# Gate and up products taken apart for the first and the last unrolled expert of a layer, and the output stored from two queues

## The reference

```
eid, gate = hier_route(x2, w_rg, b_rg, w_re, b_re)      # 32 experts, two for each token
# per expert e, on the rows routed to it:
h = silu(xb @ w_gate[e]) * (xb @ w_up[e])               # 1024 -> 512, twice
y = h @ w_down[e]                                       # 512 -> 1024
out[token] += gate * y
```

## Time and profile before

| | us |
|---|---|
| median of 3 runs (1221.98 to 1224.28) | 1223.4 |
| the profiled execution | 1221.46 |
| its span in the profile | 1219.7 |
| TensorE busy | 956.4 (78%) |
| VectorE busy | 231.7 (19%) |
| ScalarE busy | 171.5 (14%) |
| mean rate of the transfers | 360 GB/s |

### The profile page before, as it was taken

One profiled execution on the slowest core, in us unless ns is written; L12 is line 12 of the kernel. 1 busy time (PEld: TensorE's weight loads), 2 busy tenths in 40 slices (PEclk: granted clock), 3 DMA queues, 4 the chain that ended last, 5 costly groups with the idle time before them and its releaser, 6 DMA issues.

```text
span 1219.7 us, 19625 instructions
## 1 busy us (share of the span) xinstructions
PE 956.4 (78%) x8853; PEld 585.5 (48%) x8853; DVE 231.7 (19%) x765; ACT 171.5 (14%) x470; POOL 35.3 (3%) x43
## 2 busy tenths in 40 slices
PE   6997898858668676767899989996768677757576
PEld 3453566525345454544454454663535354535353
DVE  1233422111011111101120361421111011111111
ACT  1131211101011010101120261110101001101011
POOL 3311000000000000000000010000000000000000
PEclk9998999878778888878899989898878779879787
DMA  9965569999999999999983325499999999999995
GB/s 296 361 250 202 206 269 426 428 426 426 426 428 427 427 426 428 426 428 427 391 306 138 138 91 239 193 427 426 427 426 427 427 427 427 427 427 427 427 426 242
DMA packets 45731, 439.66 MB, mean 360 GB/s; under 512 B 4472, under 2 KB 5616, under 8 KB 21072
## 3 DMA queue, kind: packets, MB, share of 16 engines
q1 hardware_dynamic: 43760, 434.49, 85.8%
q0 software_dynamic: 1088, 2.97, 1.0%
q10 hardware_dynamic: 800, 0.94, 0.3%
HBM read 437.34 MB, written 1.05 MB: 359 GB/s over the span
## 4 chain that ended last, share of the span: by engine, by line
PE 50%; DMA 43%; DVE 3%; another core or an unknown queue 2%; ACT 1%; issue 1%; SPq 0%; DVEq 0%
PE psum L1218 45%; DMA mem<-in_moe_w_up 41%; PE psum L1323 3%; DMA mem<-in_ev_w_in 2%; PE psum L1225 1%; PE psum L1315 1%; DVE mem L884 1%; ACT mem L646 0%; DVE mem L1208 0%; DVE mem L1019 0%; ACT mem L596 0%; DVE mem L1023 0%; DVE x L802 0%; DVE x L972 0%
## 5 line engine op out<-in xcount | busy, mean ns | idle before, releaser
L1218 PE MATMUL psum<-mem 128*32 128x256 f32 (+4 forms) x6832 | 681.7, 450 | 220.2 <-DMA mem<-in_moe_w_up 206.7
L1218 PEld LDWEIGHTS psum<-mem 128*32 128x32 f32 (+3 forms) x6832 | 350.4, 133 | 523.8 <-issue 425.4
L1218 PE MATMUL psum<-mem,x 128*128 128x128 f32 (+1 forms) x576 | 140.4, 408 | 10.6 <-DVE mem L884 7.2
L1218 PEld LDWEIGHTS psum<-mem,x 128*128 128x128 f32 x576 | 138.4, 334 | 12.4 <-DVE mem L884 8.2
L929 DVE TENSOR_TENSOR mem<-psum,mem 128x128 f32<-128x128 f32 x62 | 18.1, 292 | 625.5 <-ACT mem L610 625.5
L610 ACT ACTIVATE mem<-psum 128x128 f32<-128x128 f32 x62 | 17.2, 277 | 472.2 <-PE psum L1218 472.2
L1323 PE MATMUL psum<-mem 32*128 32x256 f32 x1024 | 73.3, 400 | 2.9 <-ACT mem L616 2.0
L1323 PEld LDWEIGHTS psum<-mem 32*128 32x128 f32 x1024 | 46.3, 184 | 31.1 <-issue 23.9
L892 DVE TENSOR_SCALAR mem<-cst,mem 128x128 f32<-128x128 f32 x124 | 37.2, 342 | 20.7 <-PE psum L1315 20.6
L586 ACT ACTIVATE mem<-psum,g_moe 128x128 f32<-128x128 f32 x64 | 18.2, 368 | 129.7 <-PE psum L1218 129.7
L616 ACT COPY mem<-psum 128x256 f32<-128x256 f32 x62 | 23.1, 372 | 88.9 <-PE psum L1218 88.9
(11 more groups left out here) (150 smaller groups left out, 310.3 us busy)
## 6 DMA issues: line engine op xcount, KB each, us to landing
mem<-in_moe_w_gate SPq DMA_DIRECT2D x64, 2048.0 KB, 47.1
mem<-in_moe_w_up SPq DMA_DIRECT2D x64, 2048.0 KB, 45.8
mem<-in_moe_w_down SPq DMA_DIRECT2D x64, 2048.0 KB, 42.9
mem<-in_od_w_in SPq DMA_DIRECT2D x6, 2048.0 KB, 22.3
mem<-in_ev_w_in SPq DMA_DIRECT2D x3, 2048.0 KB, 30.7
mem<-in_ev_w_out SPq DMA_DIRECT2D x2, 2048.0 KB, 25.3
mem<-in_od_w_out SPq DMA_DIRECT2D x2, 2048.0 KB, 19.7
mem<-in_ev_w_in SPq DMA_DIRECT2D x2, 1024.0 KB, 8.9
```

Of the source, the lines that this page charges most:

```text
L1218: return nc.tensor.matmul(out_, lhsT, rhs, start=start, stop=stop)
```

## The change

For the experts numbered 0 and 30 in the unrolled order (the first and the last) TensorE computes the gate product alone as soon as the gate matrix is there, then does the combine of the expert before (not for expert 0) and the transposes of the gates, then waits for the up matrix and computes the up product. Each half counts `used[ph]` by one. The halves are 64 records each with 128 columns streamed instead of 64 with 256. All other experts are as before. The output transfers of groups 1 and 3 are issued by ScalarE, behind its two copies, those of groups 0 and 2 by SyncE.

```diff
+APART = (0, STATIC - 1)
...
-            for g in range(QUAD):
-                sp.wait_ge(ms[1]["final_a" if g % 2 else "final_v"], g // 2 + 1)
+            for g in (0, 2):
+                sp.wait_ge(ms[1]["final_v"], g // 2 + 1)
                 sp.dma_start(out[0].rearrange("(t p) d -> p t d", p=P)[:, :, g * COLS:(g + 1) * COLS],
                              acc(g)[1]).then_inc(s_out, 16)
...
             moe("D", 1)
+            for g in (1, 3):
+                act.wait_ge(ms[1]["final_a"], g // 2 + 1)
+                act.dma_start(out[0].rearrange("(t p) d -> p t d", p=P)[:, :, g * COLS:(g + 1) * COLS],
+                              acc(g)[1]).then_inc(s_out, 16)
+            act.wait_ge(s_out, 64)
...
+                def one_half(j, w_slot, k, ready=None):
+
+                    for r in ORDER_R:
+                        if ready is not None:
+                            ready(r)
+                        for g in range(QUAD):
+                            last = mm(bank(4)[g * CAP:(g + 1) * CAP, j * P:(j + 1) * P], xT_m[:, r, k * CAP:(k + 1) * CAP],
+                                      w_slot[:, r * FF + g * P:r * FF + (g + 1) * P], r == ORDER_R[0], r == ORDER_R[-1])
+                    return last
+
...
                     pe.wait_ge(*arrived[ph, n])
-                    pe.wait_ge(*arrived[ph, n + 1])
-                    gate_up(piece_slot(ph, n), piece_slot(ph, n + 1), k,
-                            chunk_ready if k == 0 else None).then_inc(used[ph], 5 if e == LOOP_AT else 2)
+                    if e in APART:
+                        one_half(0, piece_slot(ph, n), k, chunk_ready if k == 0 else None).then_inc(used[ph], 1)
+                    else:
+                        pe.wait_ge(*arrived[ph, n + 1])
+                        gate_up(piece_slot(ph, n), piece_slot(ph, n + 1), k,
+                                chunk_ready if k == 0 else None).then_inc(used[ph], 5 if e == LOOP_AT else 2)
                     if e not in (0, LOOP_AT):
                         pe.wait_ge(s["y"], e)
                         pe.wait_ge(s["gtc"], e)
                         combine()
                     pe.wait_ge(s["gsel"], 2 * (e + 1))
                     gates_T().then_inc(s["gtp"], 1)
+                    if e in APART:
+                        pe.wait_ge(*arrived[ph, n + 1])
+                        one_half(1, piece_slot(ph, n + 1), k).then_inc(used[ph], 1)
                     if k == QUAD - 1 and e + 1 != LOOP_AT:
                         gather_quad(q + 1)
```

## The result

The changed kernel takes 1216.68 us in the median of 7 runs (1211.06 to 1218.42), the kernel before 1223.4 us beside it (7 runs, 1221.98 to 1224.61). The ratio is 0.9943 with a 95% interval of 0.9931 to 0.9954, so 0.6% faster. The forecast was 1216.0 us with a range of 1214.4 to 1221.8. The single times spread over 7.4 us where those of before spread over 2.6.

The account below looks back on a forecast made before the run. The weight transfer stream was taken to bound both mixtures, with TensorE following. Earlier stream start 2.8, last expert 4.4 and output 0.2 us sum to 7.4, taking the median 1223.4 to 1216.0 us, range 1214.4 to 1221.8.

Parts of the forecast that it names:

- What bounds the kernel: Both mixtures: expert weights stream in at one rate, 426 to 428 GB/s, and TensorE follows the transfers.
- The half's duration: First expert of each layer: a product of half width takes 2.2 us, between 1.95 and 3.66.
- the first release: Expert 0's gate matrix is given back 1.4 us earlier (0 to 1.7), 2.8 us for the two layers.
- What the split costs expert 0: Everything hanging on expert 0's result comes 1.2 us later, which costs nothing because the stream has cover.
- The hole between the first and second piece: Sign of a wrong forecast: a gap in transfers at a stream's start; issues 2.6 us apart, first transfer 4.9 us.
- The last expert: End of each mixture: down product starts earlier, capped by its matrix's landing; 2.24 and 2.3 us, taken as 4.4.
- The clock: Rival: TensorE idling before last down product lowers clock; one end lost leaves 3.1 to 5.2 us, both about 1; chance 0.32.
- The output: Kernel's end: issuing output transfers from two queues saves 0.2 us (0 to 0.6), since the write rate limits them.
- The sum: Whole kernel: 2.8 + 4.4 + 0.2 = 7.4 us gained, from the median 1223.4 to 1216.0 us.
- Halves as dear as whole products: Rival at the split experts: a half costs 3.66 us, 57 ns a pair; gain 4.5 us, 1218.9; chance 0.12.
- dearer pairs: Rival at the split experts: half-width pairs cost over 57 ns, no gain left at 75 ns; chance 0.07.
- The stream pausing later: Rival in the weight streams: the earlier release brings nothing; gain 4.6 us, 1218.8; chance 0.03.

Follow-up runs that it names:

- e11: The changed kernel with every unrolled expert taken apart except number 16, output on two queues; 1222.39 us against 1222.38 for the kernel before, ratio 0.9993.
- e1: Only the first unrolled expert of each layer taken apart, last expert and output as in the kernel before; 1219.72 us against 1222.79, ratio 0.997.
- e2: Same TensorE work as e1, but gate and up slots given back together after the up half; 1223.02 us against 1222.79 for the kernel before.
- e5: The changed kernel again, unaltered, for its single times and one more trace; 1216.32 us against 1223.65 for the kernel before, ratio 0.9946.
- e3: Only the last unrolled expert of each layer taken apart, first expert and output as in the kernel before; 1222.02 us against 1222.79, ratio 0.999.
- e4: Only the output transfers split over two queues, no expert taken apart; 1221.91 us against 1222.79 for the kernel before, ratio 0.9996.

## Why the prediction was right, and where it wasn't

- **What bounds the kernel.** Right. The 24 streams of twelve traces (all but e11's) last 424.3 to 425.0 us whatever stands around them, and e1 and e2, the same work with another release, differ by 3.3 us.
- **The half's duration**, 2.2 us forecast between 1.95 and 3.66. It is 1.96, the lower end: 64 pairs of load and product in 1.96 us are 31 ns each. The step that failed is the 2.0 us for the load path with 0.2 us of tail behind it. The 0.125 us of a cluster had been read from a product in which the loads only needed to be done within 0.21 us; in the half the same 64 loads keep the path busy 1.7 us. Whether loads or streaming set the pace now isn't shown, since both fill the half. So the first release is 1.70 us earlier instead of 1.4, and the two layers give 3.4 instead of 2.8; e1 measured 3.1.
- **What the split costs expert 0.** Forecast 1.2 us later for all that hangs on its result; it is 0.55 (4.27 against 3.72), and costs nothing, as said. The hole between the first and second piece did not open (issues 2.25 us apart).
- **The last expert.** The mechanism and the cap are right: the down product starts 0.04 us behind the landing. With 0.12 forecast, the term is 2.40 and 2.37 us where the clock holds (e5; the latter with the output's 0.07), 4.7 instead of 4.4.
- **The clock.** The fall is commoner than forecast, and cheaper. It had a chance of 0.32; of the four traces with the whole gap open, that of the changed kernel, e3 and e11 had it, e5 alone did not, and e3's median is 0.8 us under before where 4.6 were to be had. The prices of single products were right: the down product at half rate was to lose up to 1.7 us and lost 1.67 (3.65 - 1.98), the transposes up to 1.7 and lost 1.66. The price of an end was not. With both ends lost the prediction left 1 us of 7.4, 1222.4; the first profile has both lost and gave back 1.35 and 1.36 us, since the clock fell in the middle of the down product and was back before the transposes. Only e3's layer 0 came near the forecast, 3.3 us (10.22 - 6.92). So the measured median lies below the 1218.2 to 1222.4 us of that rival. The new idle time is 2.9 us, not 2.6, since the half was shorter; I took that shorter half, as a possibility, for the lower end of the range and did not carry it into the rival.
- **The output.** 0.2 us forecast, 0.07 in the trace, no measurable time (e4).
- **The sum.** 7.4 us were forecast and 6.7 measured. With the terms as measured it would be 3.4 + 4.7 + 0.1 = 8.2 us with the clock held, 1215.2; a loss of 1.4 us at each end, as in the first profile, would give 1218. The median lies between, which fits executions of both kinds; but only two were profiled, and other stages spread as much. That the forecast came so close is luck: two terms too small and one loss left out nearly cancel.
- **The rivals that fell.** Halves as dear as whole products, and dearer pairs: 31 ns excludes both. It also speaks against the 81 ns that the Trainium skill ("TensorE: Matmul & The Clock Gate", section "Back-to-back issue gap") gives for N=128; in column tiles and float32 the measurement decides. The stream pausing later: 424.4 us excludes it.

## What to carry to other kernels

Where a transfer stream sets the time, look for the one release that starts it and for the work behind its last landing; a product that gives back its operand after half of its time moves the whole stream. The same split in the middle won nothing here, and with it the streams became longer, for a cause that stays open. When TensorE's work before a landing is made shorter, ask how long it will then idle: here, behind an idle time of 2.9 us, the clock took back 2.7 us of the 4.8 won at the two ends in one trace and about all of it in another, and 20 products of no use (2.2 us of work) won it back. Read such a change in several traces and between events, since one trace can show either case.

## What the runs showed of the hardware that had not been expected

- A product of 128 rows by 32 columns of weights and 128 streamed columns takes 31 ns with its load (64 in 1.96 us), about half of the 57 ns with 256 columns.
- The clock fell after TensorE had already begun to work again: in the first profile the down product started at 1204.58 at full clock, and the clock fell between 1205.57 and 1206.57.
- The time to layer 0's first product varies from 157.73 to 160.91 us over thirteen traces, with the same instructions ahead of it; the single times of the kernel before spread over 2.6 to 5.7 us.
- At the end of layer 1's stream, with nothing queued behind it, the last 6 to 10 us run at half of the rate or less. Eight of the last matrix's 16 parts arrive on average 5.5 us ahead of the other eight in the trace of the kernel before, and 8.2 us ahead in e11's.
